# Gate and up products of a SwiGLU as one 2x2 block product in seven half products instead of eight

## The reference, cut to what matters

```python
def swiglu(x, w_gate, w_up, w_down):
    return (jax.nn.silu(x @ w_gate) * (x @ w_up)) @ w_down
...
        x = layer_norm(DN_ALPHA * x + 0.5 * swiglu(x, ffn1_w_gate[i], ffn1_w_up[i], ffn1_w_down[i]),
                       ln_g[i, 0], ln_b[i, 0])
...
        x = layer_norm(DN_ALPHA * x + y, ln_g[i, 1], ln_b[i, 1])
        x = layer_norm(DN_ALPHA * x + mem_cross_attention(x, mem, xattn_w_q[i], xattn_w_kv[i], xattn_w_o[i]),
                       ln_g[i, 2], ln_b[i, 2])
        x = layer_norm(DN_ALPHA * x + 0.5 * swiglu(x, ffn2_w_gate[i], ffn2_w_up[i], ffn2_w_down[i]),
                       ln_g[i, 3], ln_b[i, 3])
```

## Time and profile before

| | us |
|---|---|
| median of 3 runs | 2250.05 (2249.63 to 2250.18) |
| the profiled execution, its span | 2248.1 |
| PE busy | 2225.6 (99%) |
| POOL busy | 1125.7 (50%) |
| ACT busy | 843.5 (38%) |
| DVE busy | 699.3 (31%) |
| matmuls | 10918 |

### The profile page before, as it was taken

How to read it: one execution, slowest core, us unless ns; L and a number is a source line. 1 busy time by engine, 2 the same in 40 slices (tenths; PEclk the granted TensorE clock), 3 DMA queues, 4 the chain that set the end, 5 groups by cost and what they waited for, 6 DMA issues and landing times.

```text
span 2248.1 us, 27934 instructions
## 1 busy us (share of the span) xinstructions
PE 2225.6 (99%) x10918; PEld 1843.5 (82%) x10918; DVE 699.3 (31%) x1447; ACT 843.5 (38%) x1445; POOL 1125.7 (50%) x723
## 2 busy tenths in 40 slices
PE   9999999999999999999999999999999999999998
PEld 7888888878888888888888888887778888888886
DVE  2111116465344111114310111646655344101115
ACT  3322224563445222223422222467654444322223
POOL 4454445567547444444644444445548555444443
PEclk9999999999999999999999999999999999999999
DMA  5332323213413333333333232221004312332321
GB/s 190 94 102 87 102 91 117 84 48 113 142 38 113 104 102 92 98 100 91 102 102 94 93 104 86 93 76 29 20 11 131 104 57 94 96 102 88 108 90 62
DMA packets 57874, 204.91 MB, mean 91 GB/s; under 512 B 6928, under 2 KB 7056, under 8 KB 57232
## 3 DMA queue, kind: packets, MB, share of 16 engines
q1 hardware_dynamic: 56016, 197.68, 28.5%
q10 hardware_dynamic: 1728, 5.45, 0.7%
HBM read 201.01 MB, written 2.10 MB: 90 GB/s over the span
## 4 chain that ended last, share of the span: by engine, by line
PE 97%; DVE 1%; ACT 1%; POOL 1%; issue 0%; DMA 0%; ACTq 0%; DVEq 0%
PE bank L1375 26%; PE bank L1377 26%; PE bank L1376 26%; PE bank L1708 2%; PE bank L1669 2%; PE bank L1641 1%; PE bank L1642 1%; PE bank L1394 1%; PE bank L1405 1%; PE bank L1470 1%; PE bank L1472 1%; PE bank L1471 1%; PE bank L1402 1%; POOL w_lo L497 0%; PE bank L1826 0%
## 5 line engine op out<-in xcount | busy, mean ns | idle before, releaser
L497 POOL TENSOR_TENSOR w_lo<-w_raw,w_hi 128x1024 fp32r<-128x1024 f32 (+1 forms) x378 | 893.4, 2368 | 891.7 <-ACT w_hi L676 891.4
L1375 PE MATMUL bank<-x_hi,w_hi 128*128 128x512 f32 x1568 | 612.8, 391 | 2.6 <-DVE h_lo L1179 2.6
L1376 PE MATMUL bank<-x_lo,w_hi 128*128 128x512 f32 x1568 | 611.1, 390 | 0.0
L1377 PE MATMUL bank<-x_hi,w_lo 128*128 128x512 f32 x1568 | 610.9, 390 | 0.0
L676 ACT ACTIVATE w_hi<-w_raw 128x1024 fp32r<-128x1024 f32 (+1 forms) x379 | 391.4, 1036 | 522.7 <-PE bank L1377 492.4
L1375 PE MATMUL bank<-h_hi,w_hi 128*128 128x512 f32 x960 | 379.6, 395 | 2.5 <-DVE h_lo L1179 1.1
L1376 PE MATMUL bank<-h_lo,w_hi 128*128 128x512 f32 x960 | 373.9, 389 | 0.0
L1377 PE MATMUL bank<-h_hi,w_lo 128*128 128x512 f32 x960 | 373.9, 389 | 0.0
L1377 PEld LDWEIGHTS bank<-x_hi,w_lo 128*128 128x128 f32 x1568 | 294.6, 188 | 61.7
L1375 PEld LDWEIGHTS bank<-x_hi,w_hi 128*128 128x128 f32 x1568 | 294.6, 188 | 60.9 <-DVE h_lo L1179 2.9
L1376 PEld LDWEIGHTS bank<-x_lo,w_hi 128*128 128x128 f32 x1568 | 294.8, 188 | 58.0
(11 more groups left out here) (242 smaller groups left out, 2510.8 us busy)
## 6 DMA issues: line engine op xcount, KB each, us to landing
w_raw<-w_dram SPq DMA_DIRECT2D x315, 512.0 KB, 3.6
w_raw<-w_dram SPq DMA_DIRECT2D x64, 448.0 KB, 3.2
f<-mem_dram ACTq DMA_DIRECT2D x3, 1024.0 KB, 5.1
out_dram<-t SPq DMA_DIRECT2D x8, 256.0 KB, 2.2
t<-x_dram SPq DMA_DIRECT2D x2, 512.0 KB, 6.8
f<-cmp_w_dram ACTq DMA_DIRECT2D x1, 1024.0 KB, 9.3
t<-x_dram ACTq DMA_DIRECT2D x2, 256.0 KB, 5.4
t<-x_dram ACTq DMA_DIRECT2D x1, 512.0 KB, 8.1
```

What stands on the lines that cost most here:

```text
L497: pool.tensor_tensor(w_lo[:, slot(s), 0:n * P], w_raw[:, s % RAW, 0:n * P], w_hi[:, slot(s), 0:n * P].bitcast(F32), ALU.subtract).then_inc ...
L1375: pe.matmul(dst, w_hi[:, slot(s), w], m_hi[:, k, :], start=k == 0, stop=False)
L1376: pe.matmul(dst, w_hi[:, slot(s), w], m_lo[:, k, :], start=False, stop=False)
L1377: last = pe.matmul(dst, w_lo[:, slot(s), w], m_hi[:, k, :], start=False, stop=k == n - 1)
```

## The change

Pairs 0 to 2 of each FFN stage (WHOLE = 3) stay as they are. Pairs 3 to 21, 19 of 22, become a `Group`: gate and up slab are the two columns of a 2x2 block matrix of weights (its rows are the chunks 0 to 3 and 4 to 7 of the inner dimension), x is cut in the same two rows and in two halves of the tokens. The four blocks of the result (gate and up, each for 256 tokens) come from seven half products instead of eight, after the scheme of Strassen in Winograd's form. A half product is `quarter`: 4 chunks, three matmuls of 128x256 each, so 12; a group has 84 of them where a pair had 48 of 128x512.

What it takes beside PE. On x, once a stage: four differences of 128x1024 (`differences`, DVE), rounded by ACT (`comb_round`) and with rests by DVE (`comb_rest`). On the weights, for each group: four sums of 128x512 of the raw slabs (`sums_first`, `sums_second`, DVE), their rounding in two pieces of 1024 (`pair_round`, ACT) and their rests (`pair_rest`, DVE); the gate slab itself is rounded by ACT (`gate_round`) with its rest on POOL (`gate_rest`), and half of the up slab by ACT (`up_round`) and DVE (`up_rest`). On the results: ACT copies three intermediate sums out of PSUM (`keep1`, `keep2`, `keep3`, 128x256 into mkf), DVE adds them to other banks (`first`, `up2`, `up1`, 128x256), and the SiLU is in two halves (`silu_first`, `silu_second`). The results of group g are finished while group g + 1 is worked. POOL's `feed`, and ACT's, leave out the grouped slabs, and go on with the 8 down slabs. The tiles of the memory attention are used for mkf meanwhile, so they are loaded and split again behind each stage in MEMORY.

PE's order is in the last hunk: `prod1(g)`, `prod2(g)`, `prod3` of the group before, `prod6(g)`, `prod4` of the group before, `prod7(g)`, `prod5(g)`; at the end of a part `prod3` and `prod4` of its last group are worked between the first chunks of the down slabs 0 and 1. Each waits: `prod1` for `gate_lo`, `prod2` for `hidden` of the group before, `prod3` for `snap3` (`keep3`) and `pair_lo`, `prod6` for `snap1` (`keep1`), `prod4` for `up2_out`, `prod7` for `first_out`, `prod5` for `snap2` (`keep2`).

```diff
+WHOLE = 3
...
+            def gate_rest(g):
+                pool.wait_ge(gate_hi, g.count + 1)
+                hi, lo = w_gate(g)
+                pool.tensor_tensor(lo, raw(g.gate), hi.bitcast(F32), ALU.subtract).then_inc(gate_lo, 1)
...
+                feed(st.up[0][WHOLE - 1][1])
+                if st.ln == 0:
+                    masks()
+                gate_rest(st.groups[0][0])
                 for part in range(len(FPARTS)):
-                    for n, (gate, up) in enumerate(st.up[part]):
-                        feed(up + 2)
-                        if st.ln == 0 and part == 0 and n == 4:
-                            masks()
-                        if st.ln == 0 and part == 1 and n == 1:
-                            memory_split(1)
-                        if part == 0 and st.ln - 1 not in KEEPS and st.ln and n >= 2 and n < 6:
-                            if n == 2:
-                                pool.wait_ge(x_ready, KC * (st.ln + 1))
-                            base(st, 2 * (n - 2))
-                            base(st, 2 * (n - 2) + 1)
-                    for s in st.out[part]:
-                        feed(s + 3)
+                    for g in st.groups[part]:
+                        if g.next:
+                            gate_rest(g.next)
+                    feed(st.out[part][-1])
+                    if part + 1 < len(FPARTS):
+                        gate_rest(st.groups[part + 1][0])
...
+                def gate_round(g):
+                    landed(act, g.gate)
+                    if g.i:
+                        act.wait_ge(m2, g.count)
+                    elif g.part:
+                        act.wait_ge(slab_done, plain(st.out[g.part - 1][4]))
+                    else:
+                        act.wait_ge(slab_done, plain(st.s0 + 4))
+                    act.activation(w_gate(g)[0], raw(g.gate), ACT.Copy).then_inc(gate_hi, 1)
...
+                begin = st.groups[0][0]
+                feed(st.up[0][WHOLE - 1][1])
+                gate(0)
+                comb_round(2, 1)
+                hi(0, 0)
+                gate(1)
+                comb_round(3, 2)
+                hi(1, 0)
+                comb_round(4, 3)
+                pair_round(begin, 0)
+                gate(2)
+                gate_round(begin)
+                pair_round(begin, 1)
+                hi(2, 0)
+                act.wait_ge(slab_done, plain(st.s0 + 5))
+                comb_round(1, 0)
+                up_round(begin)
+                for part, mine in enumerate(st.groups):
+                    before = None
+                    for g in mine:
+                        if before:
+                            keep3(before)
+                        keep1(g)
+                        if g.next:
+                            gate_round(g.next)
+                        if before:
+                            silu_second(before)
+                        keep2(g)
+                        if g.next:
+                            pair_round(g.next, 0)
+                            pair_round(g.next, 1)
+                        if before:
+                            hi(before.pair, before.first)
+                        silu_first(g)
+                        if g.next:
+                            up_round(g.next)
+                        before = g
+                    feed(st.out[part][0])
+                    keep3(before)
+                    feed(st.out[part][1])
+                    silu_second(before)
+                    feed(st.out[part][2])
+                    hi(before.pair, before.first)
...
+                def sums_first(g):
+                    landed(dve, g.up)
+                    if g.count:
+                        dve.wait_ge(pair_lo, 2 * g.count)
+                    dve.tensor_tensor(wsum[:, 1024:1536], raw_half(g.up, 0), raw_half(g.up, 1), ALU.add).then_inc(wsum_ready, 1)
+                    landed(dve, g.gate)
+                    dve.tensor_tensor(wsum[:, 512:1024], raw_half(g.gate, 0), raw_half(g.up, 0),
+                                      ALU.add).then_inc(wsum_ready, 1)
...
+                def up1(g):
+                    dve.wait_ge(snap2, g.count + 1)
+                    dve.wait_ge(m4, g.count + 1)
+                    dve.tensor_tensor(bank_b(g)[:, half[0]], snaps(g, 1), bank_b(g)[:, half[0]], ALU.add).then_inc(up1_out, 1)
+                    dve.wait_ge(up1_out, g.count + 1)
+                    hid(g.pair, bank_b(g)[:], -0.5)
...
+                begin = st.groups[0][0]
+                if st.ln:
+                    dve.wait_ge(x_full, kept(st, KC - 1))
+                differences(1)
+                differences(2)
+                differences(3)
+                whole(0)
+                lo(0, 0)
+                comb_rest(2, 0)
+                differences(4)
+                whole(1)
+                lo(1, 0)
+                comb_rest(3, 1)
+                sums_first(begin)
+                sums_second(begin)
+                comb_rest(4, 2)
+                whole(2)
+                pair_rest(begin, 0)
+                pair_rest(begin, 1)
+                lo(2, 0)
+                comb_rest(1, 3)
+                up_rest(begin)
+                for part, mine in enumerate(st.groups):
+                    before = None
+                    for g in mine:
+                        if before:
+                            up2(before)
+                        if g.next:
+                            sums_first(g.next)
+                        first(g)
+                        if g.next:
+                            sums_second(g.next)
+                            pair_rest(g.next, 0)
+                        if before:
+                            up1(before)
+                        if g.next:
+                            pair_rest(g.next, 1)
+                        if before:
+                            lo(before.pair, before.first)
+                        if g.next:
+                            up_rest(g.next)
+                        before = g
+                    up2(before)
+                    up1(before)
+                    lo(before.pair, before.first)
...
+            def quarter(dst, w, i, moving, begin, done):
+                hi, lo = w
+                m_hi, m_lo = moving
+                for k in range(4):
+                    c = slice(512 * i + P * k, 512 * i + P * k + P)
+                    pe.matmul(dst, hi[:, c], m_hi[:, k, :], start=begin and k == 0, stop=False, skip_group_check=True)
+                    pe.matmul(dst, hi[:, c], m_lo[:, k, :], start=False, stop=False, skip_group_check=True)
+                    last = pe.matmul(dst, lo[:, c], m_hi[:, k, :], start=False, stop=k == 3, skip_group_check=True)
+                last.then_inc(done, 1)
...
+                def prod7(g):
+                    if g.n == 0:
+                        pe.wait_ge(comb_lo, c0 + 2)
+                    pe.wait_ge(first_out, g.count + 1)
+                    quarter(bank_b(g)[:, half[0]], w_pair(g, 0), 1, comb[3], False, m7)
...
+                    before = None
+                    for g in st.groups[part]:
+                        prod1(g)
+                        prod2(g)
+                        if before:
+                            prod3(before)
+                        prod6(g)
+                        if before:
+                            prod4(before)
+                        prod7(g)
+                        prod5(g)
+                        before = g
+                    out_slab(st, part, 0, range(0, 3))
+                    prod3(before)
+                    out_slab(st, part, 0, range(3, 5))
+                    prod4(before)
+                    out_slab(st, part, 0, range(5, nf - 1))
+                    out_slab(st, part, 1, range(0, 3))
+                    out(st, part, {0: nf - 1, 1: 3})
```

More of the change, by code:

```diff
@@ L417, in build, with plain, same_slot @@
         block = ctx.enter_context(nc.Block())
-        def slot(s):
-            return s % SLOTS
+        ffns = [st for st in stages if st.kind == "ffn"]
+        grouped = {}
+        turned_slot = {}
+        for st in ffns:
+            for g in sum(st.groups, []):
+                grouped[g.gate], grouped[g.up] = g, g
+            for part in st.out:
+                for j, s in enumerate(part):
+                    turned_slot[s] = (st.s0 + j) % SLOTS
+        def slot(s):
+            return turned_slot.get(s, s % SLOTS)
+        def plain(s):
+            return s + 1 - len([x for x in grouped if x <= s])
+        def same_slot(s):
+            return max((x for x in range(s) if x not in grouped and slot(x) == slot(s)), default=None)
         def wait_lo(engine, s):
@@ new lines, in pair_round @@
+                def pair_round(g, second):
+                    act.wait_ge(wsum_ready, 4 * g.count + 3 + second)
+                    if g.i >= 2:
+                        act.wait_ge((m7, m3)[second], g.count - 1)
+                    elif g.i == 1:
```

(9 more changed lines are left out.)

381 lines of the change are left out of this document (281 added, 100 removed).

## The result

The changed kernel takes 2269.13 us in the median of 4 runs (2267.14 to 2270.15), the kernel before, timed beside it, 2249.84. The ratio is 1.0085 with a 95% interval of 1.0074 to 1.0097: 0.85% slower, where 2264 and "slower" were forecast, in a range of 2232 to 2288. The profiled execution has a span of 2265.0 us (forecast 2262.5) and took 2267.14, so 2.1 us lie around it.

The account below looks back on a forecast made before the run. PE bounds the kernel, busy 2225.6 of 2248.1 us. -61.9 + 33.2 + 1.6 + 19.7 = -7.4, and +21.8 for the clock, give a span of 2262.5, with 1.95 around it 2264; range 2232 to 2288.

Parts of the forecast that it names:

- PE's work: PE's matmuls: a group takes 10.07 us where a pair took 10.88; over 76 pairs -61.9 us.
- The steady chain: Between groups: chains of 7.7 and 9.4 us leave 0.8 and 0.5 us in hand; PE waits for nothing, 0.
- The end of a part: First down slab of a part, rounded late by ACT: PE loses 3.0 us 4 times, 2.65 8 times, +33.2.
- The h_lo of the last pair: End of parts of 7 pairs: wanted after 2.72 us, comes after 2.92; 8 x 0.2 = +1.6.
- The start of a stage: PE waits at prod1 and prod7: 5.0 us in three later stages, 4.7 in stage 0, +19.7.
- The clock: Granted clock falls to 0.50 for 3.3 us behind 14 new pauses, 1.56 us each: +21.8.
- The nearest row of before, 2.61: Kernel before, until 1506.95: PE waited 2.61 us, then 3.3 us ran at clock 0.50; each fall costs 1.56.
- D: Rival: smaller waits, if POOL does not hold sums or ACT reaches the down slab earlier; 2212 to 2242, chance 0.17.
- C: Rival: the steady chain misses its 0.5 us in hand; 2283, maybe 2305; chance 0.15.
- B: Rival: the waits come, but the clock stays up after most of them; 2243 to 2250, chance 0.17.
- F: Rival: the new products miss the forecast pace; at 0.125 us each +32, 2296; chance 0.03.

Follow-up runs that it names:

- the doses: Changed kernel with one more ACT copy in each group that has a successor, behind up_round: 128x512, 2280.97 us; 1024 columns, 2298.27 us.
- the first experiment: Changed kernel with ACT rounding down slab 0 of a part earlier, ahead of hi and silu_first of the last groups: 2224.62 us, ratio 0.9885.
- the reordered start: Changed kernel with, at stage starts, DVE's first of the first group earlier and ACT's second SiLU and gate rounding ahead of pair_round: 2262.26 us, ratio 1.0056.
- the kernel with both edits: Changed kernel with down slab 0 earlier on ACT, stage start reordered, and first group's silu_first and keep3 ahead of pair roundings: 2211.20 us, ratio 0.9828.

## Why the prediction was right, point by point

**PE's work: right.** (The forecast's own figures, 0.81 us for 76 pairs, give 61.6 us, not 61.9.) Two steady groups after each other in the changed kernel, POOL's `gate_rest` and then, on DVE, the third sum:

```profile
869.54 2.62 POOL L649 TENSOR_TENSOR w_lo<-w_raw,w_hi 128x1024 fp32r<-128x1024 f32 x1 [7.48 <-ACT w_hi L867]
879.62 2.64 POOL L649 TENSOR_TENSOR w_lo<-w_raw,w_hi 128x1024 fp32r<-128x1024 f32 x1 [7.46 <-ACT w_hi L867]
```

```profile
870.13 2.56 DVE L1434 TENSOR_TENSOR f<-f,w_raw 128x512 f32<-128x512 f32 x1
```

879.62 - 869.54 = 10.08 us a group, where 10.07 was forecast. The pace of the other 128x256 matmuls carried over, and the rival that it does not fell. So the 76 pairs cost 61.6 us less. The sum at 870.13 took 2.56 us and ended 0.53 us after POOL (869.54 + 2.62 = 872.16), as in the earlier trace rows (0.56).

**The steady chain: right, and thinner than was said at one place.** No wait in it, as forecast, with 0.5 us in hand forecast and 0.43 measured with the doses. But the limit is the loop over ACT's own list, which the working did not have, and at the second groups of parts PE does wait.

**The end of a part: right.** 12 waits, 4 x 3.03 + 8 x 2.65 = 33.3 us above the pace; forecast 33.2. Forecast was 0.10 us for a slower second matmul within this; it comes on top with 0.08.

**The h_lo of the last pair: right.** It shows as 0.12 + 0.11 us at eight places, 1.9 us; forecast 1.6. (The forecast gives no working for its 2.92 us.)

**The start of a stage: right.** 1.35 + 3.85 us three times and 0.52 + 4.43 once, 20.6; forecast 1.4 + 3.6 and 0.6 + 4.1, 19.7. (Its terms give 3.7 and not 3.6, and the two for stage 0 were taken without a sum; there the first wait is at `prod2`.)

**The clock: the mechanism right, the number of falls wrong.** This is the term that was mis-sized. It was forecast to fall at 14 of 16 places, 21.8 us; it fell at 9, and the matmuls there took 15.3 us more. These windows of the changed kernel lie behind two pauses of 2.50 us and behind a stage start (52.00); PEclk is the third number from the end:

```profile
918.50:921.50 3.00, 3.00 (x18) 2.61 (x18) 0.00 (x0) 0.00 (x0) 1.75 (x1) 1.00 0.62 166
1292.30:1295.70 3.40, 3.40 (x9) 2.67 (x8) 0.00 (x0) 0.00 (x0) 1.59 (x1) 0.50 0.68 196
...
52.00:55.30 3.30, 3.30 (x17) 3.30 (x17) 2.86 (x4) 2.83 (x4) 0.00 (x0) 0.50 0.68 228
```

All eight pauses of 2.9 us and more had a fall behind them, and one of the eight of 2.50. The nearest row of before, 2.61, was read as if a pause of this length always did it. At that same wait, in a sublayer between the FFN stages, the clock fell in 9 of the 10 profiled executions of this study, so the row was a fair one for its place and no guide for another.

**What was missing, and luck.** Two more waits of 0.31 and 0.85 us at the second groups of two parts of stage 4, about 0.2 us at the second groups of the eight parts of 7 pairs, 0.08 to 0.10 at each restart: 5 us, and some 2 more that lie in no one place. They and the clock's 6.5 too many nearly cancel: the span came out 2.5 us above the forecast, and the median of the runs lies 2 us above the profiled run. The waits were forecast well, term by term; that the whole came out this close is in part luck, for with the right number of falls the forecast would have been 2256 and 9 us too low in span.

**The rivals.** D (smaller waits, a faster kernel) fell for this kernel, but what it named, ACT at the down slab earlier, is the edit of the first experiment, and that kernel is 25 us faster than the one before. C (overrun of the steady chain) did not happen; the doses show that 0.4 us more would have started it. B was half true: of the eight pauses of 2.50 us, seven kept the clock. F did not happen: the groups came at 10.08 us.

## What to carry to other kernels

Work taken off the bound engine comes back as the waits of the first and last piece of each run, where the pipeline of the others has no neighbour to hide under. Cost these ends one by one from the order in which each engine's list is written, and count what every step there is queued behind. Here the steady part gave 62 us; the ends took 56 of them and the clock behind the ends 15 more. One call that was moved gave 44 back.

## What the runs showed of the hardware

The fall of the clock is no function of the pause alone. Counted over the changed kernel and seven of the others (all but the one with the fill), at PE's waits of over 1 us in FFN stages, the first 10 us of the program left out: after 1.1 to 1.6 us none of 22; after 2.1 us or 2.0 us four of five; after 2.5 us 23 of 44, in the same places of the program in one kernel and not in another; after 2.9 us 18 of 20; after 3.7 us and more all 16. In the changed kernel each fall costs 1.4 to 2.4 us. Which pauses have one differs from kernel to kernel: with the 512 copy it is 14 places in FFN stages, in the changed kernel 9. So the times of the reordered start and of the 512 copy are to be read with their falls.

The fill in the waits is a gain by itself: a kernel in which PE must wait 2.5 to 4 us anyway ran 0.75% faster (2252.06 against 2269.13) with matmuls of no use in the wait.

The hold of DVE by POOL goes with the order and not with one operation: in the kernel with both edits it moved at the start of stage 3 from a sum to `lo`, which took 2.89 us there (732.89), also with both inputs in SBUF. The Trainium skill, page "SBUF — State Buffer", section "Who interferes with whom", states that a DVE instruction with two SBUF inputs contends with a GpSimd one that reads SBUF. These runs agree (2564 against 683 ns), and show a price here: the changed kernel is 12.7 us faster without POOL's work beside the groups, 9.7 of them shorter waits on `first`, and none of it behind the second group of a part.
